# The down product of the prompt's rows as seven block products

## The reference

```
u = h @ w_up                       # 1088 x 5632
c = conv_b + conv_w[0]*u[t-2] + conv_w[1]*u[t-1] + conv_w[2]*u[t]
a, b = split(c)                    # 2816 channels each
x = x + (gelu(a) * b) @ w_down     # 1088 x 2816 by 2816 x 1024
y = rmsnorm(x, norm_f_g)
```

## Time and profile before

| | us |
|---|---|
| median of 3 runs | 1913.81 |
| lowest, highest | 1911.7, 1914.21 |
| the profiled execution | 1909.32 |
| its span in the profile | 1906.8 |
| PE busy | 1782.7 |
| DVE busy | 1131.6 |
| ACT busy | 794.3 |
| POOL busy | 251.0 |

### The profile page before, as it was taken

One profiled execution on the slowest core, in us unless ns is written; L12 is line 12 of the kernel. 1 busy time (PEld: TensorE's weight loads), 2 busy tenths in 40 slices (PEclk: granted clock), 3 DMA queues, 4 the chain that ended last, 5 costly groups with the idle time before them and its releaser, 6 DMA issues. The chain is left out here.

```text
span 1906.8 us, 32200 instructions
## 1 busy us (share of the span) xinstructions
PE 1782.7 (93%) x12290; PEld 1522.5 (80%) x12290; DVE 1131.6 (59%) x1935; ACT 794.3 (42%) x1479; POOL 251.0 (13%) x321
## 2 busy tenths in 40 slices
PE   7999999999778887998988999999999999899997
PEld 5777779999445556666668889999999999788875
DVE  5224575443374896666668269677777776445455
ACT  4220013433773585433332144455555554334343
POOL 0000000000100302333200002133223222000000
PEclk9999999999887789999989999999999999999998
DMA  6477742431802927999946335122232222756564
GB/s 233 173 267 266 267 160 73 137 114 48 221 4 67 327 93 273 396 386 386 386 171 213 139 124 175 56 80 68 69 102 69 69 71 86 251 184 204 186 214 137
DMA packets 169826, 331.13 MB, mean 174 GB/s; under 512 B 35769, under 2 KB 97098, under 8 KB 167306
## 3 DMA queue, kind: packets, MB, share of 16 engines
q1 hardware_dynamic: 143242, 193.58, 30.9%
q0 software_dynamic: 26432, 135.50, 19.7%
HBM read 283.02 MB, written 95.68 MB: 199 GB/s over the span
## 5 line engine op out<-in xcount | busy, mean ns | idle before, releaser
L3067 PE MATMUL tl_ps<-tl_dn,tl_f 128*128 128x512 f32 x1144 | 263.5, 392 | 6.5 <-DVE tl_f L2768 4.8
L3067 PEld LDWEIGHTS tl_ps<-tl_dn,tl_f 128*128 128x128 f32 x1144 | 216.4, 190 | 53.2 <-DVE tl_dn L2764 6.5
L3001 PE MATMUL tl_ps<-tl_T_hi,tl_slots 128*128 128x272 f32 x1216 | 211.5, 288 | 1.2 <-ACT tl_u L2453 1.2
L3001 PEld LDWEIGHTS tl_ps<-tl_T_hi,tl_slots 128*128 128x128 f32 x1216 | 175.4, 188 | 1.5 <-ACT tl_u L2453 1.5
L3001 PE MATMUL tl_ps<-tl_X_hi,tl_slots 128*128 128x272 f32 x912 | 161.1, 288 | 0.7 <-ACT tl_u L2522 0.7
L2764 DVE TENSOR_TENSOR tl_dn<-all_lead,tl_dn 128x1024 fp32r<-128x1024 f32 x66 | 80.9, 1225 | 134.9 <-ACT tl_dn L2531 134.9
L763 PE MATMUL fr_ps<-fr_w_hi,h_hi 128*128 128x512 f32 x384 | 152.5, 397 | 2.4 <-DVE h_lo L547 2.4
L763 PE MATMUL fr_ps<-fr_w_lo,h_hi 128*128 128x512 f32 x384 | 151.6, 395 | 0.0
L763 PE MATMUL fr_ps<-fr_w_hi,h_lo 128*128 128x512 f32 x384 | 149.9, 390 | 0.0
L2531 ACT ACTIVATE tl_dn<-all_lead 128x1024 fp32r<-128x1024 f32 x66 | 70.0, 1060 | 159.3 <-PE tl_ps L3067 139.6
L3001 PEld LDWEIGHTS tl_ps<-tl_X_hi,tl_slots 128*128 128x128 f32 x912 | 132.1, 188 | 0.9 <-ACT tl_u L2522 0.9
(11 more groups left out here) (384 smaller groups left out, 3736.4 us busy)
## 6 DMA issues: line engine op xcount, KB each, us to landing
all_lead<-in_w_down SPq DMA_DIRECT2D x66, 512.0 KB, 3.6
out_s<-in_cache POOLq DMA_DIRECT2D x8, 4080.0 KB, 17.8
pg_pages<-in_pool POOLq DMA_DIRECT2D x64, 256.0 KB, 6.3
pg_pages<-in_pool SPq DMA_DIRECT2D x64, 256.0 KB, 7.2
pg_odds<-in_pool SPq DMA_DIRECT2D x64, 256.0 KB, 8.0
all_lead<-in_w_up SPq DMA_DIRECT2D x26, 512.0 KB, 4.7
zs<-fr_zt SPq DMA_DIRECT2D x48, 256.0 KB, 3.7
fd<-tl_c POOLq DMA_DIRECT2D x22, 544.0 KB, 4.9
```

The lines of the kernel that those rows point to most:

```text
L3001: last = pe.matmul(ps[:, (bank + n) * 512:(bank + n) * 512 + SIDE // 2], w[:, k, :], h[:, k, n * SIDE // 2:(n + 1) * SIDE // 2], start=(fi ...
L3067: last = pe.matmul(down_bank(m), x, w[:, h * 512:h * 512 + 512], start=(k == 0 and q == 0), stop=(k == FT - 1 and q == len(passes) - 1), s ...
```

## The change

The rows of the prompt (1024 x 2816) times the down weights (2816 x 1024) become seven block products: rows, channels and columns are each cut in two, giving row blocks A11, A12, A21, A22 of 512 rows by 1408 channels and weight blocks B11 to B22 of 1408 by 512. Sums of gated rows (S1 to S4) and of weights (T1 to T4) are formed first, and each product runs over FH = 11 channel tiles and four row tiles of 128. There are 77 steps in the order P1, P6, P2, P5, P3, P7, P4. The 64 sample rows are multiplied plainly, beside P1, P2, P5 and P3: `first_samples` and `samples_part`, four 128x512 matmuls per channel tile in all, into two PSUM banks of their own.

- Weight sums: in the front's units VectorE does 22 parts (`sum_part`), up to four in a unit, each of four dependent adds of 128x256. POOL's queue loads a part (512 KB in two DMAs, chunks of 1 KB) into one of two buffers and stores it (512 KB) to `td` in DRAM; a buffer is loaded again once its store has landed. `load_unit` comes behind the store of every fourth part.
- Gated sums: for tiles 0 to 10 one difference, for tiles 11 to 21 three (`add_sums`), made by VectorE inside the next unit. POOL's queue reads back what it needs and stores the results to `sd`. `last_tap` of the second half now waits for these sums too.
- The weight sums of the up units move from POOL to VectorE.
- Down steps: a step is 128x512 of rows and 128x512 of weights in one buffer of 128x1024. There are four raw buffers and a ring of 11 for the split ones. A ring buffer is free when PE has done the step 11 before. `x2` comes back tile by tile at steps 5 to 13.
- The banks are added to up to three quarters of `x2` each (`add_out`, 44 adds of 128x512). P1's are also copied by ScalarE to `kept`, P6's are added to that. VectorE does this for block q behind the rest of step 11(q+1)+5. The last block, P4, runs row tile by row tile, with a norm and a store behind each. The stores of the first five tiles are issued by POOL.

The diff, cut to its core, the first eight columns of indent left out:

```
+FH = FT // 2
...
+    w_parts = a["w_down"].rearrange("(q k p) (n h c) -> k h q p n c", q=2, p=P, n=2, c=256)
+    def load_part(i):
+        if i >= 2:
+            pool.wait_ge(wsum_stored[i % 2], 16 * (i // 2))
+        for q in range(2):
+            pool.dma_start(wsum[:, i % 2, q, :, :], w_parts[i // 2, i % 2, q]).then_inc(wsum_in[i % 2], 16)
+    def store_part(i):
+        pool.wait_ge(wsum_step, 4 * i + 4)
+        pool.dma_start(td[i // 2, :, :, (i % 2) * 256:(i % 2) * 256 + 256],
+                       wsum[:, i % 2, :, :, :].rearrange("p q n c -> p (q n) c")).then_inc(wsum_stored[i % 2], 16)
...
     load_unit(1)
...
-        load_unit(s_)
+    pool.wait_ge(lo_made, 7)
+    load_unit(2)
+    pool.wait_ge(t_lo_done, 3)
+    load_part(0)
+    load_part(1)
+    for i in range(2 * FH):
+        if 1 <= i < 2 * FH - 1:
+            load_part(i + 1)
+        store_part(i)
+        if i % 4 == 3 and 3 + i // 4 < NU:
+            pool.wait_ge(lo_made, 7 * (2 + i // 4))
+            load_unit(3 + i // 4)
...
+    def sum_part(i):
+        x = wsum[:, i % 2, :, :, :]
+        dve.wait_ge(wsum_in[i % 2], 32 * (i // 2 + 1))
+        dve.tensor_tensor(x[:, 1, 1, :], x[:, 1, 1, :], x[:, 0, 1, :], ALU.subtract).then_inc(wsum_step, 1)
+        dve.wait_ge(wsum_step, 4 * i + 1)
+        dve.tensor_tensor(x[:, 0, 1, :], x[:, 0, 1, :], x[:, 0, 0, :], ALU.subtract).then_inc(wsum_step, 1)
+        dve.wait_ge(wsum_step, 4 * i + 2)
+        dve.tensor_tensor(x[:, 0, 0, :], x[:, 0, 0, :], x[:, 1, 1, :], ALU.add).then_inc(wsum_step, 1)
+        dve.wait_ge(wsum_step, 4 * i + 3)
+        dve.tensor_tensor(x[:, 1, 0, :], x[:, 1, 0, :], x[:, 0, 0, :], ALU.subtract).then_inc(wsum_step, 1)
+    def sum_parts(s_, at):
+        if 4 * s_ + at < 2 * FH:
+            sum_part(4 * s_ + at)
...
         more = s_ + 1 < NU
         finish_c22(s_)
+        sum_parts(s_, 0)
         if more:
             unit_rest(s_ + 1, "A12")
             unit_rest(s_ + 1, "S3")
             sum_s2(s_ + 1)
+            sum_parts(s_, 1)
             unit_rest(s_ + 1, "S2")
             sum_s1(s_ + 1)
             unit_rest(s_ + 1, "S1")
             sum_s4(s_ + 1)
         finish_c12(s_)
+        sum_parts(s_, 2)
         if more:
             unit_rest(s_ + 1, "A22")
             finish_c11(s_ + 1)
             unit_rest(s_ + 1, "S4")
+        sum_parts(s_, 3)
...
+step_raws = [x.rearrange("p (u d) -> p u d", u=2)[:, u, :] for x in (raw1[:, :, :].rearrange("p k r -> p (k r)"), raw[:, :])
+             for u in range(2)]
+ring = [ring_a[:, 2], ring_a[:, 3], ring_a[:, 0], *(ring_t[:, i] for i in range(8))]
...
+TILES = (0, 1, 2, 3, QT, 4, 5, 6, 7)
+FIRST = 5
+DOWN = ("P1", "P6", "P2", "P5", "P3", "P7", "P4")
+STEPS = len(DOWN) * FH
+LEAD = 5
+NORMS = ((0, 5), (5, 6), (6, 7), (7, 8), (8, 9))
 LAST = 2 * ((UNITS - 1) % 2)
-RING = [2 - LAST, 3 - LAST, 6, 7, LAST, LAST + 1, 4, 5]
+TURNS = (2 - LAST, 3 - LAST, 6, 7, 4, 5)
+S_BANKS = (LAST, LAST + 1)
...
     def load_step(n):
...
+        q, k = divmod(n, FH)
+        name, landed, to = DOWN[q], step_in[n % 4], step_raws[n % 4]
+        if n < 4:
+            sp.wait_ge(lo_made, 7 * (UNITS - 1 + n // 2))
         else:
...
+            sp.wait_ge(step_lo, n - 3)
+        block, sum_no = {"P1": (0, None), "P2": (1, None), "P4": (1, None), "P5": (None, 0), "P6": (None, 1), "P7": (None, 2),
+                         "P3": (None, 3)}[name]
+        if sum_no is None:
+            sp.wait_ge(f_stored, 16 * (block * FH + k + 1))
+            sp.dma_start(to[:, 0:512], fd[block * FH + k][:, HALF2 if name == "P4" else HALF1]).then_inc(landed, 16)
         else:
...
+            sp.wait_ge(sums_stored, 16 * (k + 1 if name == "P7" else sums_made(FH + k)))
+            sp.dma_start(to[:, 0:512], sd[sum_no, k]).then_inc(landed, 16)
+        if name in ("P1", "P2", "P3"):
+            r0, c0 = (0 if name == "P1" else FH) + k, 512 if name == "P3" else 0
+            sp.dma_start(to[:, 512:1024], a["w_down"][r0 * P:r0 * P + P, c0:c0 + 512]).then_inc(landed, 16)
+        else:
+            sp.dma_start(to[:, 512:1024], td[k, :, ("P6", "P5", "P4", "P7").index(name), :]).then_inc(landed, 16)
...
         if n == 4:
...
+            sp.wait_ge(tap, 8 * (FT - 1))
+            sp.wait_ge(beside, 8 * (FT - 1))
+            load_samples(0)
+        if 5 <= n < 5 + RT:
+            if n == 5:
+                sp.wait_ge(p_ready, made("P3", UNITS - 1, UNITS))
+            t = n - 5
+            sp.dma_start(x2[0:rows_of(t), t, :], x2d[t * P:t * P + rows_of(t), :]).then_inc(x2_back, 16)
...
+        load_step(n)
...
+    def store_difference(j):
+        pool.wait_ge(sum_step, sums_made(j))
+        pool.dma_start(sd[2, j], s4[:, :]).then_inc(sums_stored, 16)
+    def load_sums(j):
+        k = j - FH
+        pool.wait_ge(sums_stored, 16 * sums_made(j - 1))
+        pool.wait_ge(f_stored, 16 * (k + 1))
+        pool.dma_start(sums[:, 0, :], sd[2, k]).then_inc(sums_in, 16)
+        pool.dma_start(sums[:, 1, :], fd[k][:, HALF2]).then_inc(sums_in, 16)
+    def store_sums(j):
+        n, k = sums_made(j - 1), j - FH
+        pool.wait_ge(sum_step, n + 1)
+        pool.dma_start(sd[1, k], sums[:, 0, :]).then_inc(sums_stored, 16)
+        pool.wait_ge(sum_step, n + 2)
+        pool.dma_start(sd[0, k], sums[:, 1, :]).then_inc(sums_stored, 16)
+        pool.wait_ge(sum_step, n + 3)
+        pool.dma_start(sd[3, k], s4[:, :]).then_inc(sums_stored, 16)
...
+    for j in range(FH):
         store(j)
-    sum_s3(0)
-    sum_s2(0)
-    sum_s1(0)
-    sum_s4(0)
...
-    sum_s3(1)
-    for s_ in range(UNITS):
-        if s_ + 1 < UNITS:
-            sum_s2(s_ + 1)
-            sum_s1(s_ + 1)
-            sum_s4(s_ + 1)
-        if s_ + 2 < UNITS:
-            sum_s3(s_ + 2)
...
+        store_difference(j)
+    pool.wait_ge(u_ready, 2 * PLAIN_UP)
+    for j in range(FH, FT):
+        load_sums(j)
+        store(j)
+        store_sums(j)
...
+    def step_head(n):
+        act.wait_ge(step_in[n % 4], 32 * (n // 4 + 1))
         step_room(act, n)
...
+        act.activation(ring[n % FH][:, 0, :], step_raws[n % 4], ACT.Copy).then_inc(step_hi, 1)
...
+    def keep(r):
+        act.wait_ge(out_ready, r + 1)
+        act.activation(kept[:, r, :], down_bank(r), ACT.Copy).then_inc(bank_kept, 1)
...
+    def add_sums(j, part):
+        if j < FH:
+            if part == 0:
+                dve.wait_ge(f_done, j + 1)
+                if j:
+                    dve.wait_ge(sums_stored, 16 * j)
+                dve.tensor_tensor(s4[:, :], c[:, 1, HALF1], c[:, 1, HALF2], ALU.subtract).then_inc(sum_step, 1)
+        elif part == 0:
+            dve.wait_ge(f_done, j + 1)
+            dve.wait_ge(sums_in, 32 * (j - FH + 1))
+            dve.tensor_tensor(sums[:, 0, :], c[:, 1, HALF2], sums[:, 0, :], ALU.subtract).then_inc(sum_step, 1)
+        elif part == 1:
+            dve.tensor_tensor(sums[:, 1, :], c[:, 1, HALF2], sums[:, 1, :], ALU.add).then_inc(sum_step, 1)
+        else:
+            dve.wait_ge(sum_step, sums_made(j - 1) + 1)
+            dve.tensor_tensor(s4[:, :], c[:, 1, HALF1], sums[:, 0, :], ALU.subtract).then_inc(sum_step, 1)
...
     for s_ in range(UNITS):
         j, more = PLAIN_UP + s_, s_ + 1 < UNITS
         finish_c22(s_)
         if more:
             rest(s_ + 1, "A12")
+            add_sums(j - 1, 0)
             rest(s_ + 1, "S3")
+            sum_s2(s_ + 1)
+            add_sums(j - 1, 1)
             rest(s_ + 1, "S2")
+            sum_s1(s_ + 1)
+            add_sums(j - 1, 2)
             rest(s_ + 1, "S1")
+            sum_s4(s_ + 1)
         else:
-            step_rests(0)
-            step_rests(1)
...
+            for i in range(3):
+                add_sums(j - 1, i)
+                step_rest(i)
+        tap_back(j, 1, 1)
         finish_c12(s_)
+        tap_back(j, 1, 2)
         if more:
             rest(s_ + 1, "A22")
             finish_c11(s_ + 1)
...
-            step_rests(2)
         convolve(j, 0)
         if more:
             rest(s_ + 1, "S4")
         else:
-            step_rests(3)
+            step_rest(3)
         if s_ + 2 < UNITS:
             rest(s_ + 2, "A11")
+            sum_s3(s_ + 2)
         product(j)
+    for i in range(3):
+        add_sums(FT - 1, i)
...
+        step_rest(n)
...
+        q, after = divmod(n - FH - LEAD, FH)
+        if q == 0 and after == 0:
+            dve.wait_ge(x2_back, 16 * RT)
+        if q >= 0 and after == 0:
+            for at in range(4):
+                if DOWN[q] == "P6":
+                    add_kept(at)
+                else:
+                    for quarter in QUARTERS[DOWN[q]]:
+                        add_out(DOWN[q], at, quarter)
+            if DOWN[q] in ("P2", "P3"):
+                add_samples(("P2", "P3").index(DOWN[q]))
+        if q == 1 and 1 <= after < 7:
+            for what in [what for what in ADDS if what[0] == "P6"][2 * after - 2:2 * after]:
+                add_out(*what)
+        if n == 5 * FH + LEAD + 6:
```

(87 more changed lines are left out.)

352 lines of the change are left out of this document (168 added, 184 removed).

## The result

The changed kernel is slower, by a quarter of a percent: a median of 1918.45 us (14 runs, 1914.25 to 1924.52) against 1913.45 us (14 runs, 1909.55 to 1916.88) of the kernel before in the same session, ratio 1.0026 with a 95% interval of 1.0015 to 1.0038. The prediction was 1881 us. The profiled execution took 1921.77 us, its span 1920.1 us.

A forecast was written before the change was run, and what follows sets the result against it. TensorE, busy 93% of the span, was taken as the bound. Down steps -32.8, end -3.9, gate units +4 make -32.7 us on 1909.3: 1876.6, plus 4.5 to the median, 1881 us; range 1869 to 1902.

The forecast's parts named there:

- The ring of the front: Front's gate units: two part buffers, 9.3 us per round trip, 22.2 us per unit; 4 us cost after absorption.
- rival one: Gate units become DMA bound: 15 us at a 10.5 us trip, 32 us at 12; centre 1895 us, chance 0.20.
- The other bound: Front's gate units: DMA traffic with four parts takes 21.0 of 21.1 us of engine time per unit.
- The samples' matmuls: Down steps: sample rows need 22x2x2 = 88 matmuls, of 1012 in all, at 0.2267 us each.
- The start of the stage: Down steps: PE waits 1.9 us at step 4 for VectorE's rest 4; 2.2 us taken.
- the old wait: Down steps before: 4.8 us wait from reloading `x2` at once; dropped with its clock loss, as tiles now load separately.
- P4's first row: Last down block: 4.1 us of waits for new steps, plus 1.5 us for a possible clock loss.
- Up units: Still about 21.1 us apart, VectorE busy 17.9 us in each; cost 0 us.
- Rival three: VectorE bounds the up units: 23.3 us per unit costs 42 us, giving 1923 us; chance 0.08.
- The end: Behind the last matmul: last `y` made after 4.75 us instead of 8.6; 3.9 us less.

The follow-up runs named there:

- three_a_unit: Against the changed kernel: three weight-sum parts per gate unit instead of four, over units 0 to 7, still two buffers; 1887.86 us, ratio 0.9877.
- three_buffers: Against the changed kernel: a third buffer for the weight-sum parts, POOL storing part i before loading part i+2; 1884.09 us, ratio 0.9854 to the kernel before; repeated, 1887.20 us.
- down_b: Changed kernel plus third part buffer, rests 4 and 5 before tile 21's sums, samples and gain loaded later, P1's banks emptied behind step 14; 1877.42 us, ratio 0.9803.
- rests_first: Against the changed kernel: VectorE makes the rests of down steps 4 and 5 before the gated sums of tile 21; 1919.20 us, ratio 1.0031 to the kernel before.

## Why the prediction was wrong

- **The ring of the front, the step that failed.** "I take 9.3 us: 22.2 us per unit" for store, reload and landing. The round measured 4.94 + 6.34 + 1.28 = 12.6 us. The means give 5.6 + 5.3 + 1.4 = 12.2 us. The store was put at 3.1 us at least, its best value alone, and took 5.6; the load at 4.0 us, where two transfers of 256 KB with 0.7 us of issue each took 5.3; for traffic the 9.3 us had 1.8 us on top of both. The 1.28 us behind the other buffer's load was no term at all: for each queue I had asked what is moved past what, but not here. With 12.2 us my own formula gives 2 x (12.2 + 1.8) = 28.0 us per unit, 6.9 x 5.5 = 38 us, less 2 to 3 absorbed; 37 were measured. So the result is the far end of rival one (12 us, +32; its sum takes off 4 us where the forecast takes off 2 to 3), and `three_a_unit` and `three_buffers` show its mechanism. But its name was wrong: the units were not DMA bound, since they ran at a share of 0.70. The other bound, 21.0 of 21.1 us of engine time, was near the truth but did not decide: with three buffers the same bytes went through at a share of 0.92 and PE waited 1.9 us.
- Rival one had a chance of 0.20 with its centre at a trip of 10.5 us, although held the 6.9 and 4.9 us of transfers beside other traffic. Two parts were to pass through a chain of six serial pieces (issue, landing, adds, issue, landing, wait in the queue), and I took each near its best.
- By the Trainium skill (DMA: Bandwidth & Descriptors, "Where 436 GB/s comes from") the limit is about 358 GB/s. `down_b` moved 411 GB/s over 10 us, more than that again; the gate stretch stays below the figure even while the parts run (231 GB/s in after, 315 GB/s with three buffers), so the rule decided nothing here.
- **The samples' matmuls were miscounted.** 22x2x2 = 88 were predicted; the profile has 110, since `first_samples` does four per step beside P1, and P2, P5 and P3 have two per step each: 11 x 10. The section on the change says four per channel tile; it is five on average. The reason is in the program: the samples' product with B12 is made as that with B11 plus that with the weight sum of P5, which is B12 - B11.

```profile
L3261 PE MATMUL tl_ps<-tl_ring_t,tl_fs x80: 389/389/389, 1696.7 to 1844.4; 128*128 128x512 f32 x80
...
L3261 PE MATMUL tl_ps<-tl_ring_a,tl_fs x30: 389/389/397, 1685.8 to 1819.1; 128*128 128x512 f32 x30
```

22 x 0.2267 = 5.0 us too little: 1034 x 0.2267 = 234.4 us. The rate itself held.
- **The start of the stage**: a wait of 2.2 us was predicted at step 4 for the right reason (rest 4 behind the sums of tile 21), but with the sums' load taken as landed. It landed after 8.4 us, and the wait was 5.2 us. `rests_first` and `down_b` show that more was hidden: 10 us of issues ahead of step 11 in SP's queue (7.3 us in after), which the walk left out. In PE's restart at 1680 to 1684 the granted clock is 0.50, the 1.2 GHz level; I had dropped this clock loss with the old wait.
- **P4's first row** was too dear: 4.1 us of waits and 1.5 of clock predicted; 1.8 us recorded, the longest 1.3, and some 0.9 more in steps 1.14 us apart where 0.68 would do, at full clock. So the 8.6 us of the stage are +5.0 of matmuls, +3.0 at step 4, some 3 of clock and 0.4 for a bank, less the 2.9 by which P4 cost less than predicted. In `down_b`, 237.3 us come near the 237.2 predicted, but by luck: 5.0 us more of matmuls, 2.9 less in P4 and the 2.2 of the start's wait, which that kernel no longer has, cancel.
- **Up units right**: unchanged, VectorE at 326.4/19 = 17.2 us per unit against 17.9 predicted. Rival three, the slower one by VectorE, did not come: the kernel is slower for another reason than the one I had named.
- **The end right**: 3.5 us less against 3.9.

```profile
1905.02 5.60 PE L3251 MATMUL tl_ps<-tl_ring_t 128*128 128x512 f32 x24
...
1913.95 1.28 DVE L2960 SCALAR_TENSOR_TENSOR tl_y<-tl_x,tl_rstd,tl_gain_f 128x1024 f32<-128x1024 f32 x1
```

The last of these matmuls ends at 1910.6, `y` at 1915.2: 4.6 us against the 4.75 predicted.

The saving was real: with the ring repaired (`three_buffers`) the kernel is 1.45% faster than before, 1884 to 1887 us against the 1881 predicted. That this is near is partly luck too: its down steps take 245 us as in after, and the kernel's piece between gate and up units varies by more than the difference. The 37 us in the front took all of it and 5 us more.
